# A six-layer transformer kernel in split fp32r: one order of steps per engine in the last two layers, inverse roots from exponentials, split scores, and three slots for the split weights

## The reference

```python
proj = rms_norm(x, norm_g) @ w_in                       # 3104 columns
a, a_glu, z_conv, c_q, c_kv, k_rope, z_mla, u_sg, v_sg, z_sg = split(proj)
y_conv = silu(layer_norm(causal_conv31(a * sigmoid(a_glu)) + conv_b)) @ pw_w + pw_b
y_conv = y_conv * silu(z_conv)
q = rms_norm(c_q, g) @ w_uq; kv = rms_norm(c_kv, g) @ w_ukv     # 8 heads
q = rope(rms_norm(q, qk_q_g)); k = rope(rms_norm([k_nope, k_rope], qk_k_g))
y_mla = causal_softmax(q @ k.T / sqrt(96)) @ v * silu(z_mla)
y_sg = gelu(u_sg) * (tril(sg_w) @ layer_norm(gelu(v_sg)) + sg_b) * silu(z_sg)
x = x + [rms_norm(y_conv), rms_norm(y_mla), rms_norm(y_sg)] @ w_out
```

## Time and profile before

| | us |
|---|---|
| median of 3 runs (lowest, highest) | 1706.46 (1704.57, 1707.08) |
| the profiled execution's own time | 1706.29 |
| its span, first to last instruction | 1704.5 |
| mean granted clock of TensorE | 0.963 of 2.4 GHz |

### The profile page before, as it was taken

One profiled execution on the slowest core, in us unless ns is written; L12 is line 12 of the kernel. 1 busy time (PEld: TensorE's weight loads), 2 busy tenths in 40 slices (PEclk: granted clock), 3 DMA queues, 4 the chain that ended last, 5 costly groups with the idle time before them and its releaser, 6 DMA issues. The chain is left out here.

```text
span 1704.5 us, 21913 instructions
## 1 busy us (share of the span) xinstructions
PE 1535.2 (90%) x9045; PEld 1325.4 (78%) x9045; DVE 963.8 (57%) x1177; ACT 802.8 (47%) x1170; POOL 164.0 (10%) x165
## 2 busy tenths in 40 slices
PE   7977999999889999888999998789999787699777
PEld 6755899987779998767999886569998676587666
DVE  5554654465655445654544555445555487667755
ACT  6446444344344434533443454454444454655463
POOL 2000000000000000000000000000000296008800
PEclk9998999999999999999999999889999898999799
DMA  9212455543225554321555541225555422254220
GB/s 308 100 64 85 149 198 197 197 158 139 99 99 198 197 197 157 141 73 52 196 197 197 185 173 54 95 99 184 176 183 197 136 83 88 99 151 161 93 99 25
DMA packets 100615, 241.96 MB, mean 142 GB/s; under 512 B 2642, under 2 KB 11644, under 8 KB 100540
## 3 DMA queue, kind: packets, MB, share of 16 engines
q1 hardware_dynamic: 98848, 237.25, 39.1%
q0 software_dynamic: 1344, 3.52, 1.0%
q10 hardware_dynamic: 348, 0.13, 0.0%
HBM read 239.84 MB, written 1.05 MB: 141 GB/s over the span
## 5 line engine op out<-in xcount | busy, mean ns | idle before, releaser
L1239 DVE TENSOR_TENSOR wlo<-raw,whi 128x2048 fp32r<-128x2048 f32 (+3 forms) x240 | 511.5, 2167 | 238.1 <-ACT whi L502 237.9
L502 ACT ACTIVATE whi<-raw 128x2048 fp32r<-128x2048 f32 (+3 forms) x240 | 418.8, 1790 | 165.5 <-PE pair L863 163.1
L861 PE MATMUL pair<-whi,xhi 128*128 128x512 f32 (+2 forms) x752 | 305.3, 406 | 19.8 <-DVE xlo L1268 13.8
L861 PE MATMUL pair<-xhi,whi 128*128 128x256 f32 x1024 | 290.9, 284 | 6.9 <-DVE xlo L1268 6.9
L862 PE MATMUL pair<-wlo,xhi 128*128 128x512 f32 (+2 forms) x752 | 294.8, 392 | 0.0
L863 PE MATMUL pair<-whi,xlo 128*128 128x512 f32 (+2 forms) x752 | 294.1, 391 | 0.0
L862 PE MATMUL pair<-xlo,whi 128*128 128x256 f32 x1024 | 289.7, 283 | 0.0
L863 PE MATMUL pair<-xhi,wlo 128*128 128x256 f32 x1024 | 289.7, 283 | 0.0
L861 PEld LDWEIGHTS pair<-xhi,whi 128*128 128x128 f32 x1024 | 196.4, 192 | 10.3 <-issue 6.9
L861 PE MATMUL pair<-whi,ahi 128*128 128x512 f32 x512 | 199.8, 390 | 0.0
L862 PE MATMUL pair<-wlo,ahi 128*128 128x512 f32 x512 | 199.5, 390 | 0.0
(11 more groups left out here) (235 smaller groups left out, 1699.7 us busy)
## 6 DMA issues: line engine op xcount, KB each, us to landing
raw<-in_mlp_w_up SPq DMA_DIRECT2D x32, 2048.0 KB, 8.5
raw<-in_mlp_w_down SPq DMA_DIRECT2D x32, 2048.0 KB, 7.6
raw<-in_diff_w_in SPq DMA_DIRECT2D x11, 2048.0 KB, 8.9
raw<-in_w_in SPq DMA_DIRECT2D x10, 2048.0 KB, 7.8
raw<-in_moba_w_in SPq DMA_DIRECT2D x6, 2048.0 KB, 7.8
raw<-in_diff_w_out SPq DMA_DIRECT2D x4, 2048.0 KB, 7.8
raw<-in_w_uq SPq DMA_DIRECT2D x4, 1152.0 KB, 5.5
raw<-in_moba_w_out SPq DMA_DIRECT2D x2, 2048.0 KB, 7.7
```

The lines of the kernel that those rows point to most:

```text
L502: act.activation(whi[:, s, cols], raw[:, s, cols], ACT.Copy).then_inc(*t["hi_split"].one())
L861: pe.matmul(dst, x_hi, w_hi, start=first, stop=False)
L1239: dve.tensor_tensor(wlo[:, s, cols], raw[:, s, cols], whi[:, s, cols].bitcast(FP32), ALU.subtract)\
```

## The change

- Weights have three slots. The low part is written over `raw` (the tile `wlo` lies on the same bytes), so SP loads block j only when PE has used up block j-3. ACT and DVE no longer wait for PE before they split (`used()` becomes `passed()`, which only counts), except where they read results.
- Inverse roots: ACT takes `Ln` of the mean and `Exp` of minus half of it, both in one table set; DVE refines it by one Newton step of four small operations. The table set is loaded ahead after each use of another one.
- The MLP loops are written out.
- Second layers: each engine has a list of its own. Blocks 2 and 3, and 8 and 9, trade places. POOL only adds taps, ACT scales them into a ring of 12 buffers. POOL applies gain and bias of both layer norms. The gains of queries and keys go into the tables of rope (made by POOL) and into the scale with which a turned head is split; the query's root goes into the scale of the exponential. `prep` is done by groups of four heads. Heads are turned two at a time and split into high and low parts, and `scores` is that of the first layers (fp32r). ACT copies the turned probabilities.

```diff
-BLOCKS_2 = [..., ("w_in_2", CKV0, KT, KVL + ROPE2), ("w_in_2", ZC0, KT, 512), ("w_in_2", U0, KT, 512), uq, ukv, uq,
-            ("w_in_2", ZM0, KT, MLAW), ("w_ukv_2", 512, KVL // P, 512), ("w_in_2", ZS0, KT, SGW), pw]
+BLOCKS_2 = [..., ("w_in_2", ZC0, KT, 512), ("w_in_2", CKV0, KT, KVL + ROPE2), ("w_in_2", U0, KT, 512), uq, ukv, uq,
+            ("w_ukv_2", 512, KVL // P, 512), ("w_in_2", ZM0, KT, MLAW), ("w_in_2", ZS0, KT, SGW), pw]
...
-        def second_steps():
...
+        def tensor_steps():
+            steps = part("in", 0, 0, 8) + part("in", 1, 0, 5) + [("conv_in", 0)] + part("in", 1, 5, 8)
+            steps += part("in", 2, 0, 8) + part("in", 3, 0, 8) + part("in", 4, 0, 2) + [("latents", 0)]
+            steps += part("in", 4, 2, 8) + part("in", 5, 0, 1) + [("conv_norm", 0)] + part("in", 6, 0, 1)
+            steps += part("in", 7, 0, 1) + part("in", 8, 0, 1) + part("in", 9, 0, 3) + [("heads", 0)] + part("in", 9, 3, 8)
+            steps += [("heads", 1), ("scores", 0)] + part("in", 10, 0, 4)
+            steps += [("conv_operand", 0), ("turn", 0), ("heads", 2), ("mix", 0), ("scores", 1)] + part("in", 10, 4, 8)
+            steps += [("heads", 3), ("turn", 1), ("sgu_mix", 0), ("pw", 0), ("scores", 2), ("mix", 1), ("turn", 2), ("scores", 3), ("mix", 2), ("y", 0), ("turn", 3), ("mix", 3)]
+            steps += part("out", 0, 0, 6) + [("y", 1)] + part("out", 0, 6, 8) + part("out", 1, 0, 8)
+        def scalar_steps():
+            steps = [("split", 0), ("split", 1), ("in_results", 0), ("glu", 0), ("split", 0)]
+            steps += [("split", 1), ("conv_in", 0), ("taps", 0, 8), ("in_results", 1), ("taps", 8, 22)]
+            steps += [("split", 0), ("split", 1), ("in_results", 2), ("taps", 22, 31), ("split", 0)]
+            steps += [("split", 1), ("in_results", 3), ("split", 0), ("split", 1), ("latents", 0)]
+            steps += [("latents", 1), ("latents_root", 0), ("shared", 0), ("in_results", 4), ("gelu", 0)]
+            steps += [("split", 0), ("split", 1), ("in_results", 5), ("prepsq", 0, 0), ("in_results", 6)]
+            steps += [("split", 0), ("split", 1), ("prepsq", 1, 0), ("prep_root", 0, 0), ("conv_norm", 0)]
+            steps += [("in_results", 7), ("split", 0), ("in_results", 8), ("prepsq", 0, 1), ("prep_root", 1, 0)]
+            steps += [("split", 1), ("split", 0), ("conv_silu", 0), ("heads", 0), ("prepsq", 1, 1)]
...
+        def vector_steps():
...
+            steps += [("in_results", 10), ("split", 0), ("split", 1), ("glu", 0), ("split", 0)]
+            steps += [("split", 1), ("conv_in", 0), ("taps", 0, 18), ("split", 0), ("split", 1)]
+            steps += [("taps", 18, 26), ("split", 0), ("split", 1), ("split", 0), ("taps", 26, 28)]
+            steps += [("latents", 0), ("latents", 1), ("latents_root", 0), ("split", 1), ("taps", 28, 31)]
+            steps += [("conv_stats", 0), ("split", 0), ("split", 1), ("reduce", 0, 0), ("split", 0)]
+            steps += [("split", 1), ("reduce", 1, 0), ("prep", 0, 0), ("conv_norm", 0), ("split", 0)]
+            steps += [("v_stats", 0), ("prep", 1, 0), ("split", 1), ("split", 0), ("reduce", 0, 1)]
...
+            steps += [("split", 0), ("split", 1), ("sgu_gate", 0), ("scores", 2), ("turn", 2)]
+            steps += [("heads", 3), ("outputs", 0), ("pw", 0), ("branch_gates", 0), ("split", 0)]
+            steps += [("scores", 3), ("turn", 3), ("branches", 0), ("split", 1), ("y", 0)]
...
+            def inverse_roots(dst, log, parts, eps_at=0):
+                for (at, n, w), src in parts:
+                    m = act.activation(log[:, at:at + n], src, ACT.Ln, scale=1.0 / w, bias=eps[:, eps_at:eps_at + 1])
+                m.then_inc(*t["log_taken"].one())
+                act.wait_ge(*t["log_taken"].now())
+                return act.activation(dst[:, some], log[:, some], ACT.Exp, scale=-0.5)
...
+            def scale_taps(layer, taps):
+                    else:
+                        if k > N_TAPS:
+                            act.wait_ge(sems["tap_added"], layer * (CONV_K - 2) + k - N_TAPS)
+                        m = act.activation(scaled[k % N_TAPS], y, ACT.Copy, scale=w)
...
+            def refined(dst, x, y, factor):
+                chain(dve.tensor_tensor(factor, y, y, ALU.mult))
+                chain(dve.tensor_tensor(factor, factor, x, ALU.mult))
+                chain(dve.tensor_scalar(factor, factor, -0.5, 1.5, ALU.mult, ALU.add))
+                return dve.tensor_tensor(dst, factor, y, ALU.mult)
...
             def load(src, T, w):
-                s = t.block % 2
+                s = t.block % SLOTS
-                if t.block >= 2:
-                    sp.wait_ge(*t["lo_split"].now(2))
+                if t.block >= SLOTS:
+                    sp.wait_ge(sems["block_used"], 2 * (t.block - SLOTS + 1))
...
-                    pool.tensor_scalar(tap[:, :], y, w, None, ALU.mult).then_inc(*t["pool_step"].one())
...
+                for k in range(1, CONV_K):
+                    pool.wait_ge(sems["tap_scaled"], layer * CONV_K + k + 1)
+                    pool.tensor_tensor(yacc[:, 1, :], yacc[:, 1, :], scaled[k % N_TAPS], ALU.add)
```

More of the change, by code:

```diff
@@ new lines, in tensor_steps, with part @@
+        def tensor_steps():
+            def part(what, b, first, last):
+                return [(what, b, e) for e in range(first, last)]
+            steps = part("in", 0, 0, 8) + part("in", 1, 0, 5) + [("conv_in", 0)] + part("in", 1, 5, 8)
[6 more added lines that the diff above has]
+            steps += part("out", 0, 0, 6) + [("y", 1)] + part("out", 0, 6, 8) + part("out", 1, 0, 8)
+            return steps
@@ L599, in probs_out @@
                     act.activation(pT[:, hp % 2, 0, :], pair[p][:, 0, 0:384], ACT.Copy).then_inc(*t.emptied[p].one())
+                elif mixer == "mla":
+                    act.wait_ge(*t.filled[p].after())
+                    act.activation(pT[:, hp % 2, :, :], pair[p][:, :, 0:384], ACT.Copy).then_inc(*t.emptied[p].one())
                 else:
@@ L685, in mlp @@
                 down()
-                with act.Fori(0, 3) as i:
-                    turns(t, i, MLP_TURN)
+                for _ in range(3):
                     up(0)
@@ L1005, in scores @@
+                for rows, cols, keys in ((slice(P, 2 * P), slice(P, 3 * P), SEQ), (slice(0, P), slice(0, P), P)):
+                    for i, j in ((0, 0), (0, 1), (1, 0)):
+                        for c in range(2):
+                            parts = heads(mixer, hp, c)
+                            m = pe.matmul(pair[p][:, c, cols], parts[i][0][:, rows], parts[j][1][:, 0:keys], start=False,
+                                          stop=(i, j, keys) == (1, 0, P))
                 m.then_inc(*t.filled[p].one())
@@ L1526, in mlp @@
                 down()
-                per = dict(MLP_TURN, dve_step=2)
-                with dve.Fori(0, 3) as i:
-                    turns(t, i, per)
+                for _ in range(3):
                     up(0)
@@ L1624, in second @@
                         pw_done = t.emptied[3].now()
+                    elif what == "branch_mla":
+                        for q in range(2):
+                            dve.wait_ge(*t.emptied[outputs_at(q)].now())
+                        dve.wait_ge(*t["zsilu_ready"].now())
+                        dve.tensor_tensor(qbuf[:, :, 0:MLAW], qbuf[:, :, 0:MLAW], qkv[:, :, ZM0:ZM0 + MLAW], ALU.mult)\
+                            .then_inc(*t["branches_ready"].one())
                     elif what == "branch_gates":
@@ new lines, in _ @@
+                pool.wait_ge(*t["spread_loaded"].now())
+                for which, name in enumerate(["qk_q_g_2", "qk_k_g_2"]):
+                    for i, (table, part) in enumerate(((0, 0), (1, 1), (0, 1), (1, 0))):
+                        g = param2(name)[:, NOPE + part * HALF2:NOPE + (part + 1) * HALF2]
+                        pool.tensor_tensor(cs2g[:, which, i, :, :], cs2[:, table, :, :], lanes(g.unsqueeze(1), [P, TT, HALF2]), ALU.mult)\
+                            .then_inc(*t["rope_tables"].one())
```

562 lines of the change are left out of this document (319 added, 243 removed).

## The result

| | median, us | ratio to before, 95% interval |
|---|---|---|
| the kernel before, 4 runs | 1706.77 | |
| the changed kernel, 4 runs | 1684.24 (1683.84 to 1684.37) | 0.9865 (0.9853 to 0.9877) |
| the changed kernel on another chip, 4 runs | 1685.22 (1683.03 to 1687.35) | 0.9857 (0.9835 to 0.9880) |

The change makes the kernel 22.5 us faster where 49 us were forecast; the time lies inside the stated range of 1634 to 1692. The profiled execution took 1684.2 us.

What follows compares the result with a forecast made beforehand. PE bounds the kernel, busy 90%, with waits and lowered clock in the second layers. Terms sum to -25.1 us a layer, 2 given back: -46 for two, -3 in first layers, 1706.3 to 1657 us; range 1634 to 1692.

Steps and rivals of the forecast that it cites:

- Wait 3: PE's 8.5 us before `conv_norm`, behind POOL's last tap; gone once POOL only adds: -8.5 us per second layer.
- Wait 1: PE's 5.3 us before the first `w_uq` block, for `llo` behind 11 DVE taps; 1.3 left, net -4.0 per second layer.
- Wait 4: PE's 7.6 us before `pw`, behind `prep` and `conv_operand` on DVE; operand ready earlier: -7.6 us per second layer.
- Wait 2: PE's 2.2 us for a low part in the short blocks; becomes 4.4 at second `w_uq` and ZM0: +2.2 per second layer.
- Attention: PE's waits in the second layers' attention: six become six others, 9.7 us against 8.8, +0.9 per layer.
- Split scores: `scores` in the second layers' attention: 1.25 us split against 1.77 plain, four times, -2.1 us per layer.
- Clock: PE's half-clock loss in the second layers, taken as halved because remaining waits are short: -6 us per layer, between 0 and -11.
- First layers: Diff mixer roots: `Ln`, `Exp` and four small operations replace a table load on the path, 0.5 us six times: -3.
- Queues full: Rival, 0.22: DVE's 121 us fill three quarters of a shortened second layer, steps come late, half the gain: 1681 us.
- Slower: Rival, 0.06: POOL's adds cost 2.5 us each, so PE stands at `conv_norm` 34 us longer: 1725 us.
- More: Rival, 0.12: the clock stays up all through and first layers' attention gains: 1640 us.
- not what it says: Rival, 0.03: waits change places, to `latents` and ZM0, each as long as the old ones; time within 0.2%.

Runs made afterwards that it cites:

- pool_scales: The changed kernel with POOL again scaling the taps as well as adding them, and ACT scaling none: 1721.7 us, ratio 1.0072.
- pw_count: The changed kernel with `pw` waiting for the count recorded when the convolution's operand was split, not the newest count of that bank half: 1672.5 us, ratio 0.9809.
- busy: The changed kernel with latents' low parts earlier on DVE, `pw` waiting on its operand's own count, and four attention gaps filled with small multiplications: 1654.4 us, ratio 0.9691.
- plain_root: The changed kernel without the Newton step of the inverse roots, DVE copying ACT's exponential instead: 1668.1 us, ratio 0.9758.
- before_slots: The kernel before with only the three weight slots, low parts over the loaded weights, and written-out MLP loops: 1710.8 us, ratio 1.0006.

## Why the prediction was right or wrong

- **Sign, range, where it would show: right.** The MLP stretch is as full as before; the gain is in the second layers (26.9 us); POOL's time there fell from 76 to 41 us a layer. Of the signs named, the clock of 0.94 or above did not come (0.90 and 0.92), nor did a wait under 1 us before `pw`.
- **Wait 3 (-8.5): right.** PE didn't wait at `conv_norm`; POOL's adds came every 0.88 us beside the taps, and the 30 of the last layer took from 1535.6 to 1568.0 us, 32 where the walk allowed 40. `pool_scales` shows the other side, 25.1 us.
- **Wait 1 (-4.0): wrong, and the cause is contention read in one direction only.** The prediction asked how POOL is held up by DVE, and kept 7.50 us for 11 taps as if the taps were a constant. They had already lain beside half a dose of POOL's work. Alone a tap takes 0.484 us, beside scalings and adds 0.633, beside adds back to back 0.782. The change removed the scalings between the adds and so raised the dose. In the last layer 27 taps ahead of `llo` took 22.85 us, 5.8 more than at the 0.633 of before. Measured 5.3 and 5.7 in place of 1.3: 8.4 us over the two layers. The ring of 12 and ACT's `in_results` 3, which the walk took for the new wait, were not it. The Trainium skill, page "SBUF — State Buffer", section "SBUF: two separate sides", has a DVE instruction with two SBUF inputs share a port pair with GpSimd that whoever starts first holds "for the whole instruction" while the other fully blocks. The traces agree that the taps are held up. They don't show a full block: a tap that began 0.17 us behind an add of 0.74 lasted 0.85, where waiting the add out and then 0.48 alone would make 1.05, an estimate. Nor do the adds lose in the dense stretch: 0.74 beside taps, 0.72 with DVE idle. In the alternation of before they did lose, 0.86 beside a tap (the one at 1567.44) against 0.72 without. So the prediction's reading that the trace agrees "for the splits only" was wrong in its own rows.
- **Wait 4 (-7.6): half right.** The silu and the operand were early, as said. The walk followed data, but PE waits for counts, and this one also counts `sgu_gate`: 2.46 us remain in each layer, 4.9 in all. `pw_count` shows it.
- **Wait 2 (+4.4 in place of 2.2): right, even high.** 0.89 and 2.12 us in the last layer, 0.88 and 3.19 in the one before, released by DVE's `wlo` as walked.
- **Attention (9.7): high.** 6.0 and 5.3 us.
- **Idle time in all.** 17.0 less per layer, with the give-back 15.0, so 30 for two; measured 27.6. The sum held because errors of both signs met in it, two small waits among them that nobody had walked: for the gate (0.48 and 1.48 us) and for block 3's low part (0.69 and 1.05).
- **Split scores (-2.1): wrong size.** Here one `scores` step at full clock takes 1.67 us from its first matmul to the next step's (`busy`: 1621.68 to 1623.35), against 1.77 for a plain one: 0.1 gained, not 0.52. The 1.25 us came from the first layers, whose heads have 64 rows; these have 96. A price was carried over from another shape; that the rows are the cause was not tried.
- **Clock (-6 a layer): wrong, the largest error.** Time at half clock from 1330 us on fell only from 76.3 to 66.6 us, and weighted with PE's busy share in each 2 us it rose, from 50.1 to 52.1. At half the pace that is 1.0 us lost in place of 12 gained, an estimate. The waits that went had held spells of half clock in which PE had nothing to do; in the last layer, gaps of 2.16 and 1.63 us in the attention, one step apart, were enough for a spell of 17 us (1639 to 1656) that now lies on dense work. `busy` shows that such gaps matter beside the sum of the waits: 40 small multiplications a layer raised the clock.
- **First layers (-3): wrong by size.** About 0 at equal clock; in this profile +4.8 by clock. The Newton chain was costed at the six roots of the diff mixer only. `plain_root`, a single profile, shows some 4 us less idle time without it (93.9 for 95.9 to 99.0).
- **Slots and loops at 0: right** for the time, shown by `before_slots`.
- **The balance.** Forecast 49, measured 22.1 in the profiles' spans. Missing: 16.9 of busy time (forecast -16.2, measured +0.7), 7.8 in the first layers, 2.4 of idle time: 27.1.
- **The rivals.** "Queues full" gave 1681, the nearest number. Part of its mechanism was there: DVE is busy for 72% of the second layers (249.4 of 344.3), the three quarters it named, and `llo` came late behind a row of DVE's. But it had half of the gain lost to late steps, and the idle time fell by 27.6 of the 30 us forecast; what is missing lies in the clock and the first layers, and one edit of DVE's order removes the wait for `llo`. "Slower" asked for adds of over 2.1 us: they stayed at 0.93 on average. "More" asked for a clock that stays up, and "not what it says" for new waits as long as the old ones: neither came.

## What to carry to other kernels

When work on POOL is packed more densely, price what it does to DVE's instructions beside it as well as the reverse, from runs or rows at different densities. A wait on a shared count waits for everything that the count holds; record the value where the operand is made. And don't credit a better clock for waits that go: look at which gap stands in front of the half-clock spell, and try filling it.

## What was not expected of the hardware

- DVE's tap (`scalar_tensor_tensor`, 128x256, two inputs from SBUF) takes 0.484, 0.633 or 0.782 us on average, by what POOL does beside it, while POOL's adds in the dense stretch keep their 0.74; a split of 128x1152 in two takes 2.63 or 3.71 us.
- One gap of 2.16 us in the attention is followed by half clock for most of 24 us though PE is busy for 20 of them; with this gap and three of 0.9 us filled, there is none.
- Identical first layers take 1332.4 to 1340.0 us, with 47.6 to 68.2 us at half clock.
